# A new order of work on VectorE, SyncE and GpSimd, and the input norm's root moved to GpSimd

## What is computed

```
h = rmsnorm(x) * norm_mix_g
cv, cg, q, f, v, og, ga, gb = split(h @ w_in)              # 7168 columns
u = cv * sigmoid(cg)                                       # convolution branch
c = silu(layernorm(depthwise_conv31(state_conv ++ u)))     # 512 channels
y_a = c @ w_conv_out
fg = lb + (1 - lb) * sigmoid(f);  k = 1 - fg               # recurrent branch, 8 heads of 128
q = silu(q) * 128 ** -0.5
S_t = diag(fg_t) S_{t-1} + k_t v_t^T;   o_t = S_t^T q_t
y_b = (rmsnorm(o) * hgrn_norm_g * silu(og)) @ w_hgrn_out
x = x + (sigmoid(ga) * y_a + sigmoid(gb) * y_b) @ w_out
x = x + experts(rmsnorm(x))       # 32 experts, best group of 4, best 2 experts in it
y = rmsnorm(x)
```

## Time and profile before

| | us |
|---|---|
| median of 3 runs | 877.0 (875.82 to 877.13) |
| the profiled execution | 874.24 |
| its span | 872.4 |
| TensorE busy | 808.7 (93%) |
| VectorE busy | 261.3 (30%) |
| ScalarE busy | 155.4 (18%) |
| GpSimd busy | 109.2 (13%) |
| DMA, mean over the span | 311 GB/s |

### The profile page before, as it was taken

One profiled execution on the slowest core, in us unless ns is written; L12 is line 12 of the kernel. 1 busy time (PEld: TensorE's weight loads), 2 busy tenths in 40 slices (PEclk: granted clock), 3 DMA queues, 4 the chain that ended last, 5 costly groups with the idle time before them and its releaser, 6 DMA issues.

```text
span 872.4 us, 9412 instructions
## 1 busy us (share of the span) xinstructions
PE 808.7 (93%) x3845; PEld 472.2 (54%) x3845; DVE 261.3 (30%) x543; ACT 155.4 (18%) x240; POOL 109.2 (13%) x127
## 2 busy tenths in 40 slices
PE   6999979998199999999899999999999899999996
PEld 4888868887198888886333333333333333323332
DVE  3069986467254221234110111101110111011103
ACT  4014312423121250014111110101000010010002
POOL 4100050263143000002000000000300000000001
PEclk9999999998699999999899999999999999999998
DMA  8845546593672867238999999999999999999993
GB/s 308 263 171 204 159 141 194 169 240 73 200 238 97 335 268 288 98 133 314 371 427 428 397 424 427 427 427 427 429 424 427 427 428 425 427 427 421 421 422 123
DMA packets 74388, 271.53 MB, mean 311 GB/s; under 512 B 5606, under 2 KB 37426, under 8 KB 58975
## 3 DMA queue, kind: packets, MB, share of 16 engines
q1 hardware_dynamic: 72586, 267.65, 78.8%
q0 software_dynamic: 640, 2.16, 0.7%
q10 hardware_dynamic: 1117, 1.08, 0.4%
HBM read 259.26 MB, written 12.09 MB: 311 GB/s over the span
## 4 chain that ended last, share of the span: by engine, by line
PE 68%; DMA 19%; DVE 5%; SPq 4%; POOL 2%; issue 1%; ACT 1%; POOLq 0%; ACTq 0%; DVEq 0%
PE bank L1461 19%; PE bank L1789 17%; DMA slots<-in_w_expert_gate_dram 10%; PE bank L1827 9%; PE bank L1699 7%; PE bank L1836 5%; DMA slot<-in_w_expert_gate_dram 3%; SPq L523 3%; PE bank L1475 3%; PE bank L1646 2%; DMA list_rows<-early,list_at 1%; DMA gb<-in_state_hgrn_dram 1%; PE bank L1839 1%; DVE ga L1054 1%; DVE slot L1037 1%
## 5 line engine op out<-in xcount | busy, mean ns | idle before, releaser
L1461 PE MATMUL bank<-hT,slots 128*128 128x264 f32 x896 | 209.2, 393 | 0.7 <-DVE hT L992 0.7
L1789 PE MATMUL bank<-slots,hT 128*64 128x512 f32 x688 | 194.2, 600 | 8.4 <-DMA slots<-in_w_expert_gate_dram 8.4
L1461 PEld LDWEIGHTS bank<-hT,slots 128*128 128x128 f32 x896 | 172.2, 194 | 30.3 <-issue 1.3
L1331 DVE TENSOR_TENSOR early<-early,bank 128x512 f32<-128x512 f32 x16 | 11.0, 687 | 394.5 <-PE bank L1789 394.5
L1789 PEld LDWEIGHTS bank<-slots,hT 128*64 128x64 f32 x688 | 59.9, 138 | 110.2 <-issue 95.7
L1827 PE MATMUL bank<-slots,wrep 128*64 128x512 f32 x336 | 108.3, 602 | 5.4 <-ACT wrep L910 5.4
L1789 PE MATMUL bank<-slot,hT 128*64 128x512 f32 x256 | 76.2, 594 | 1.2 <-DMA slot<-in_w_expert_gate_dram 1.2
L727 POOL COPY hT<-early 128x512 f32 x30 | 17.6, 615 | 389.4 <-PE bank L1789 288.9
L1836 PE MATMUL bank<-hT,diag 128*128 128x512 f32 x128 | 59.2, 605 | 0.0
L1827 PEld LDWEIGHTS bank<-slots,wrep 128*64 128x64 f32 x336 | 32.8, 138 | 48.0 <-issue 40.3
L1037 DVE SCALAR_TENSOR_TENSOR slot<-slot,rows_buf 128x256 f32<-128x256 f32 x120 | 55.7, 540 | 0.0
(11 more groups left out here) (276 smaller groups left out, 765.2 us busy)
## 6 DMA issues: line engine op xcount, KB each, us to landing
slots<-in_w_expert_down_dram SPq DMA_DIRECT2D x19, 2048.0 KB, 28.2
slots<-in_w_expert_up_dram SPq DMA_DIRECT2D x18, 2048.0 KB, 28.5
slots<-in_w_expert_gate_dram SPq DMA_DIRECT2D x18, 2048.0 KB, 28.8
slots<-in_w_in_dram SPq DMA_DIRECT2D x14, 2048.0 KB, 8.7
slot<-in_w_expert_gate_dram SPq DMA_DIRECT2D x8, 2048.0 KB, 25.7
slot<-in_w_expert_up_dram SPq DMA_DIRECT2D x5, 2048.0 KB, 26.4
slot<-in_w_expert_down_dram SPq DMA_DIRECT2D x5, 2048.0 KB, 30.9
slots<-in_w_expert_gate_dram SPq DMA_DIRECT2D x8, 1024.0 KB, 21.6
```

Source lines behind the costliest of these rows:

```text
L1461: last = mm(out, w[:, a, t * P:(t + 1) * P], hT[:, a, :], start=(a == 0), stop=(a == KT - 1))
L1789: last = mm(out[sl, :], xe[:, a, sl], expert_view(p, kind, e, a // 4)[:, a % 4, :], start=(a == 0), stop=(a == KT - 1))
```

## The change

It has five parts.

1. SyncE issues the samples' rows of x ahead of the prompt's. ScalarE squares them first, and it is now ScalarE that copies the turned x out of PSUM. The root is made on GpSimd, by two small scalings and a power. TensorE spreads the root after the fourth of eight tiles instead of after all; VectorE copies it to SBUF and makes `hT` tile by tile while TensorE turns the rest. The turning of the taps moves in between the first and the second tile of the projection.
2. At the end of q, VectorE forms the samples' products from the unscaled q and scales q after them; the sums with the samples' q and k are scaled when they leave PSUM. Four taps that stood here move to later places. TensorE's `o_rows` now waits for the scaled q.
3. GpSimd's order of `decayed_qk` and `sample_head` changes.
4. VectorE's order of takes, differences and state updates changes from level 3 on.
5. SyncE's order of state loads, state stores and value loads changes.

The core of the diff:

```diff
+            sp.dma_start(xtok[0:NB, 2, :], xs).then_inc(x_in[2], 16)
             for i in range(2):
                 sp.dma_start(xtok[:, i, :], xp[i * P:(i + 1) * P, :]).then_inc(x_in[i], 16)
-            sp.dma_start(xtok[0:NB, 2, :], xs).then_inc(x_in[2], 16)
...
                     store_states(0)
                     load_values(2)
+                    wait_stored(0)
+                    load_states(2, NEW_IN[2])
                     store_states(1)
                     load_values(3)
-                    wait_stored(0)
-                    load_states(2, NEW_IN[2])
...
+            step(pool.memset(power[:, :], -0.5))
+            pool.wait_ge(x_squared, 3)
+            step(pool.tensor_scalar(rs[0:NB, 2:3], ss[0:NB, 2:3], 1.0 / D, EPS, ALU.mult, ALU.add))
+            step(pool.tensor_scalar(rs[:, 0:2], ss[:, 0:2], 1.0 / D, EPS, ALU.mult, ALU.add))
+            pool.tensor_tensor(rs[:, :], rs[:, :], power[:, :].broadcast_to([P, 3]), ALU.pow).then_inc(rms_ready, 1)
...
-            for work in (0, 1, 2, 3, "s0", "s1", "s2", "s3", 4, "s4", "s5", 5, "s6", "s7", 6, 7, 8):
+            for work in (0, 1, 2, 3, "s0", "s1", 4, "s2", "s3", 5, "s4", "s5", 6, "s6", "s7", 7, 8):
...
+            for d in range(KT):
+                se.wait_ge(misc.ready, misc.written(("x", d)))
+                se.copy(xT[:, d, :], bank[misc.bank(("x", d))][:, 0:T]).then_inc(M_act, 1)
...
             src = take(misc, "rsb")
+            dve.tensor_copy(rstd, src[:, 0:T]).then_inc(M_dve, 1)
+            dve.wait_ge(*misc.read("rsb"))
+            for d in range(KT):
+                dve.wait_ge(*misc.read(("x", d)))
+                dve.scalar_tensor_tensor(hT[:, d, :], xT[:, d, :], vec[:, d:d + 1], rstd,
+                                         ALU.mult, ALU.mult).then_inc(hmix_ready, 1)
...
-            dve.tensor_scalar(q, q, DK ** -0.5, None, ALU.mult).then_inc(q_ready, 1)
-            dve.wait_ge(q_ready, 1)
             dve.tensor_tensor(qk_own, q[:, :, SEQ:T], k[:, :, SEQ:T], ALU.mult).then_inc(own_ready, 1)
             dve.wait_ge(own_ready, 1)
-            dve.tensor_tensor(q[:, :, SEQ:T], q[:, :, SEQ:T], fgs[:, :, :], ALU.mult).then_inc(own_ready, 1)
-
-            tap(4)
+            step(dve.tensor_tensor(q[:, :, SEQ:T], q[:, :, SEQ:T], fgs[:, :, :], ALU.mult))
+            dve.tensor_scalar(q, q, DK ** -0.5, None, ALU.mult).then_inc(q_ready, 1)
             o_rows(0)
...
+            level_take(3, (0, 1))
             level_diff(6)
-            level_take(3, range(4))
-            states_add(2)
+            level_take(3, (2, 3))
...
+            states_add(2)
+            level_diff(7)
+            level_take(4, (0, 1))
+            level_take(4, (2, 3))
             states_add(4)
-            level_take(4, (0, 1))
-            level_diff(7)
-            level_take(4, (2, 3))
-            level_take(5, (0, 1))
-            states_add(6)
+            level_take(5, range(4))
             level_diff(8)
-            level_take(5, (2, 3))
             level_take(6, range(4))
...
-            for d in range(4):
-                gated_a(d)
+            gated_a(0)
+            gated_a(1)
+            states_add(6)
+            gated_a(2)
+            gated_a(3)
...
-                pe.wait_ge(own_ready, 2)
+                pe.wait_ge(q_ready, 1)
```

More of the change, by code:

```diff
@@ L1146, in _ @@
             level_diff(3)
+            tap(2)
             diag_take(3)
@@ new lines, in _ @@
+            for d in range(2):
+                turn_x(d, 1).then_inc(M_ready, 1)
+            for d in range(2, KT):
+                if d == 4:
+                    pe.wait_ge(vec_in, 16 * 9)
+                    misc.before_write(pe, "vec")
+                    tr(bank[misc.bank("vec")][:, 0:76], vecr, ident[0:76, 0:76]).then_inc(M_ready, 1)
+                    pe.wait_ge(diag_ready, 3)
+                    pe.wait_ge(c_ones, 1)
+                    misc.before_write(pe, "rsb")
+                    for i, (t0, m) in enumerate(TOK_TILES):
+                        last = mm(bank[misc.bank("rsb")][:, t0:t0 + m], ones[0:m, 0:P], diag[0:m, i, 0:m], start=True, stop=True)
+                    last.then_inc(M_ready, 1)
@@ L1430, in _ @@
                 misc.before_write(pe, ("x", d))
[L1431 to L1433 removed]
+                for i in range(3):
+                    last = turn_x(d, i)
                 last.then_inc(M_ready, 1)
[L1435 to L1437 removed]
@@ L1438, in _ @@
-            pe.wait_ge(tap_in, 16)
-            misc.before_write(pe, "taps")
-            for c in range(CT):
-                last = tr(bank[misc.bank("taps")][:, c * TAPS:(c + 1) * TAPS], tapr[:, c * P:(c + 1) * P], ident[0:TAPS, 0:TAPS])
-            last.then_inc(M_ready, 1)
-            pe.wait_ge(diag_ready, 3)
-            pe.wait_ge(c_ones, 1)
-            misc.before_write(pe, "rsb")
-            for i, (t0, m) in enumerate(TOK_TILES):
-                last = mm(bank[misc.bank("rsb")][:, t0:t0 + m], ones[0:m, 0:P], diag[0:m, i, 0:m], start=True, stop=True)
@@ L1537, in turn_rows @@
                 last.then_inc(M_ready, 1)
-            in_projection(0)
+            in_tile(0, 0)
+            pe.wait_ge(tap_in, 16)
+            misc.before_write(pe, "taps")
+            for c in range(CT):
+                last = tr(bank[misc.bank("taps")][:, c * TAPS:(c + 1) * TAPS], tapr[:, c * P:(c + 1) * P], ident[0:TAPS, 0:TAPS])
+            last.then_inc(M_ready, 1)
+            for t in range(1, 4):
+                in_tile(0, t)
             pe.wait_ge(prod_ready, 2)
```

56 lines of the change are left out of this document (21 added, 35 removed).

## The result

The changed kernel takes 841.72 us (median of 4 runs, 840.61 to 843.31), the kernel before 877.07 us beside it (4 runs, 875.82 to 877.44). The ratio is 0.9601, with a 95% interval of 0.9582 to 0.9619: 35.35 us less, where 31.1 were forecast.

A forecast was written before the change was run, and what follows sets the result against it. TensorE's waits before 400 us were taken as the bound, with nothing left in the expert stage. 0.8 + 6.9 + 4.9 + 18.5 = 31.1 us off 874.24 gave 843.1, plus 2.8 made 845.9 us; range 841 to 862.

The forecast's parts named there:

- forecast case: The whole kernel takes 843 to 849 us; chance 0.62.
- head: First tile starts up to 1.46 us earlier, less 0.60 for the taps' transposes: net 0.8 us won, bounds 0 and 0.9.
- boundary at q: TensorE's waits of 1.2 and 4.0 us and 1.7 us of slow clock go: 6.9 us won.
- expert stage: From 400 us to the end: untouched, nothing left to give; earlier wins should arrive at the end in full.
- Level 3: Near 196 us: decayed_qk(4) right after s1 cuts a cost of 6.1 us to 1.2: 4.9 won, bounds 0 and 6.1.
- The forecast's other reading: Level 3, port rule to the letter: none of states_add(0)'s sixteen get in, TensorE resumes 1.0 us later, 3.9 us won.
- Level 4: Near 221 us: level 4 ahead of states_add(4), states loaded earlier; 1.5 us wait left, 18.5 won, bounds 0 and 20.0.
- (a): Rival: the new short waits also pull the clock down, 4.9 us less won: 850.8 us, up to 857; chance 0.20.
- (b): Rival: level 4's stall moves to states_add(6), TensorE stops about 10 us at the output tiles: 857.7 us; chance 0.12.
- (c): Rival: SyncE's wait for the first states' store delays later transfers; slower than before, 877 us and more; chance 0.04.
- (d): Rival: the head does nothing because another input is last: 846.7 us, inside the forecast's range; no chance of its own.
- the offset: 2.8 us by which the median before (877.0) exceeds the profiled execution (874.24), added to 843.1 to give 845.9.

The follow-up runs named there:

- pool_old: The changed kernel with GpSimd's old order of decayed_qk and sample_head put back; 853.08 us, ratio 0.9709.
- vector_new: The kernel before with VectorE's new order alone, all else as it was; 867.17 us, ratio 0.9904.
- vector_old: The changed kernel with VectorE's old order put back alone; 864.38 us, ratio 0.9866.
- before_again: The kernel before, unedited, run again for a second profile and more times; 878.5 us, ratio 1.0004.
- head_alone: The kernel before with the changed head alone; 875.91 us, ratio 0.9980.
- q_alone: The kernel before with only the change at the end of q; 870.17 us, ratio 0.9905.
- taps_back: The changed kernel with only the four taps put back ahead of the copy of os; 845.24 us, ratio 0.9642.
- convs_later: The changed kernel with TensorE's convolution products (L1556) moved behind two more tiles, between tiles 2 and 3 of chunk 1; 840.33 us, ratio 0.9571.
- best: convs_later with the first half of level 3 taken ahead of two PSUM copies; 839.13 us, ratio 0.9581.

## Why the prediction was right, and where it was not

The forecast case occurred: all three places were cleared and nothing took their place. By its own steps, in the two profiles:

| step | forecast | between the profiles | medians of the runs with that part alone or without it |
|---|---|---|---|
| head | +0.8 | -1.1 | +1.1, +1.4 |
| boundary at q | 6.9 | 7.1 | 7.6 |
| levels 3 and 4 | 4.9 + 18.5 = 23.4 | 25.5 | 29.4 |
| expert stage | 0 | -0.8 | |
| sum | 31.1 | 30.7 | |

For the column between the profiles: TensorE begins `o_rows(0)` at 112.12, 1.1 us later than the 111.0 at which it got there before, and the tile at 123.90 6.0 us earlier; that makes 7.1 for the boundary. The cross scores are 31.5 us earlier, 25.5 more than the tile. The old costs were counted as 6.1 + 20.0 = 26.1, and the wait that is left is 0.7: 25.4. That 31.1 meets the 30.7 is in part luck: in these two profiles the head brings 1.9 us less than forecast and the levels 2.1 us more. The parts of the last column, each alone, add up to 38.4 us (1.4, 7.6 and 29.4) where the change brings 35.35; the intervals of the last two are each some 2 us wide to either side, so it stays open whether the parts overlap.

**Head: right, but past its bound.** The start of the first tile moved from 17.11 to 15.96. The forecast let the weights set it. They landed 10.3 us after their issue at 5.58, at 15.9, but TensorE was turning x until 16.0 and waited for nothing, so that they are the limit is not shown. Nor does the granted clock show that the first tile "waits for the clock": it reads 1.00 from 11 to 22 us, though some of the tile's matmuls took 0.81 us where 0.39 is usual. The two medians give 1.1 and 1.4 us where 0.9 was the most allowed; the taps take 0.43 us in their new place, not 0.60. That an earlier TensorE can run into GpSimd's L675 was not foreseen. It is small, and seen in one profile only.

**Boundary at q: right**, mechanism and size. The copy out of PSUM kept its pace beside GpSimd (0.69 us), and the displaced taps were covered.

**Level 3: right in size, partly wrong in cause.** The wait left is 0.7 us (1.2 forecast), and 0.8 to 1.2 in five other profiles with the new orders there. GpSimd's order was held to be what clears this place. pool_old and vector_new have the old one and no wait there: it is the take of the first half ahead of `level_diff(6)` that does it. What GpSimd's order brings, 11.4 us when all else is new, is at levels 4 and 6, places for which the forecast gave it nothing.

The slowing of `states_add(0)` beside GpSimd went as the taps of the earlier trace rows had said. Sixteen updates took 11.41 us from 177.55. GpSimd ran until 181.8 and from 182.65 to 186.45. At 0.27 us each, three fit the gap and nine the 2.4 us after 186.45; so four got in beside four products. The very first took 2.04 us, until GpSimd's product ended at 179.44. The Trainium skill (SBUF — State Buffer, section "SBUF: two separate sides") has the loser wait for a whole instruction. The 2.04 us agree. The forecast's other reading, that none gets in while products follow each other, goes further than that sentence. By it 13 would have been left at 186.45, for 3.5 us, to 189.9; the end is at 188.9. About one update for each boundary between two GpSimd instructions agrees with the trace.

**Level 4: right, and under-sized.** The forecast left 1.5 us of wait; there is none. The chain of transfers ran as laid out but sooner: states issued at 194.67, not 202. The covers named for ScalarE's gates and for `s6` and `s7` held: GpSimd's `s6` ran at 223.65, eight microseconds ahead of the forecast.

**The rivals.** (a) New short waits without a slow clock: 0.72 us left the pair at 2.02. The head's 0.55 us did have a tail, a place (a) did not name. (b) The stall did not move in the changed kernel: `states_add(6)` started at 242.59 with no wait. vector_old, where it is left inside level 5, shows that it was a real danger: 11.30 us. (c) SyncE's wait for the first store delayed nothing that TensorE asked for. (d) The head did something.

**What was mis-sized is the offset, and with it the stalls.** The forecast took 843.1 for the profiled execution and added the 2.8 us by which the median of before stood above its own profile. That treats the difference as something every kernel has. before_again, head_alone and q_alone show that most of it sat in the two stalls which the change removes: 21.3 us in the profile of the forecast, 24.2 to 26.3 in the other three. Without the offset the forecast is 843.1, 1.4 us from the median, and the gain is as much larger as the stalls were dearer in the median than in that profile. The profile of after erred the other way, 1.6 us above its median. The two errors together are 4.4 us, the difference between 35.35 and 30.9. Two things could make up the 1.6: the accident in the head, and the expert stage, which took 464.7 us from the transfer of the lists on in this profile and 462.3 to 464.1 in twelve others. No run separates them.

**The parts don't add up one by one.** Each order taken back alone costs 8.75 (SyncE), 11.4 (GpSimd) and 22.7 us (VectorE), 42.8 together, but all three bring 29.4. VectorE's alone brings 9.5. The other two with head and boundary (vector_old) bring 876.71 - 864.38 = 12.3, and some 9 of those are the head and the boundary (1.4 + 7.6), so the two bring some 3 by themselves. Each order taken back leaves stalls that the other two can't avoid, and VectorE's made alone bares the next one, 11.38 us inside level 5. SyncE's and GpSimd's orders were not run each by itself.

## What to carry to other kernels

Before taking out a long stall, ask what it hides: two levels further on another transfer was in time in the kernel before, where TensorE stood still for 18 us, and in vector_old, where it did not, TensorE waited 11.3 us for it. A stall that ends with a transfer differs from one execution to the next; read it in a second profile before sizing it, and don't carry over the difference between a profile and the median to a kernel that no longer has that stall. When the orders of several engines are changed together, one order undone at a time shows what each is worth there, and one alone shows what it is worth without the others; here the two differ by more than twice (22.7 and 9.5 us for VectorE's).

## What the runs showed of the hardware beyond what was expected

- The same two state loads were used 16.5 us after their issue in one execution and 17.6 in another (217.60 to 234.07, 222.15 to 239.78), and TensorE's two stalls in these executions sum to 21.3 and 26.3 us.
- Half a microsecond of waiting was followed by a granted clock of 0.63 over 4 us, where 1.95 us of matmuls with four columns each came right behind it. Waits of 0.72 to 1.17 us ahead of full level products had no such tail in six profiles (the pair took 2.02 us and the next tile 3.73 each time), nor had 2.80 us ahead of L1524 in taps_back. Waits of 2.44 us and more ahead of level products all had one (3.10 us for a pair that takes 1.95).
- In the head the first tile took from 5.02 to 6.62 us in profiles of kernels with the same program up to there.
- VectorE is not always the one that is slowed. In the changed kernel its eight updates from 201.47 took 2.18 us and the differences behind them 1.21 each, their pace alone, while GpSimd's `s4` and `s5`, begun at 202.23, took 7.30 us together (6.92 in convs_later, 6.95 in best) where such a pair takes 3.75.
